# Two phases for the channel mixers, with the output product in Strassen's form

## What is computed

```python
def sq_relu_mlp(h, w1, w2):                 # w1 1024 x 4096, w2 4096 x 1024
    return jnp.square(jax.nn.relu(h @ w1)) @ w2
...
x = x + g2[:, None, :] * sq_relu_mlp(h, w_mlp_in[layer], w_mlp_out[layer])
```

## Time and profile before

| | |
|---|---|
| median of 3 runs | 3123.59 us (3119.03 to 3125.92) |
| profiled execution, span from first to last instruction | 3121.5 us |
| its own time beside the span | not recorded separately |
| TensorE busy | 3079.6 us, 99% |
| VectorE, ScalarE, GpSimd busy | 43%, 28%, 8% |

### The profile page before, as it was taken

How to read it: one execution, slowest core, us unless ns; L and a number is a source line. 1 busy time by engine, 2 the same in 40 slices (tenths; PEclk the granted TensorE clock), 3 DMA queues, 4 the chain that set the end, 5 groups by cost and what they waited for, 6 DMA issues and landing times.

```text
span 3121.5 us, 34385 instructions
## 1 busy us (share of the span) xinstructions
PE 3079.6 (99%) x13692; PEld 2479.9 (79%) x13692; DVE 1345.3 (43%) x1578; ACT 860.8 (28%) x1027; POOL 234.9 (8%) x352
## 2 busy tenths in 40 slices
PE   7999999999999999999999999999999999999999
PEld 5788888877777888888888778866767888888887
DVE  6664333255556333333336344255455533333333
ACT  5111222222233221111225344344244212221112
POOL 1000010000011000000011010123122000000000
PEclk8999999999999999999999999999999999999999
DMA  6655565533301111111113323455241111111111
GB/s 224 202 186 198 176 232 183 194 107 112 109 17 55 54 41 54 41 53 54 40 42 105 111 89 122 147 131 134 68 105 48 52 44 54 54 40 54 43 51 54
DMA packets 144669, 302.52 MB, mean 97 GB/s; under 512 B 10257, under 2 KB 72132, under 8 KB 144580
## 3 DMA queue, kind: packets, MB, share of 16 engines
q1 hardware_dynamic: 111220, 185.90, 18.4%
q0 software_dynamic: 33360, 115.38, 11.8%
HBM read 245.93 MB, written 55.18 MB: 96 GB/s over the span
## 4 chain that ended last, share of the span: by engine, by line
PE 93%; DVE 3%; ACT 2%; DMA 1%; issue 1%; POOL 0%; DVEq 0%; ACTq 0%; SPq 0%; POOLq 0%
PE ps L1572 10%; PE ps L1571 10%; PE ps L1568 10%; PE ps L1528 8%; PE ps L1531 8%; PE ps L1534 8%; PE ps L1686 5%; PE ps L1692 5%; PE ps L1689 5%; PE ps L1964 3%; PE ps L1660 3%; PE ps L1663 3%; PE ps L1664 3%; PE ps L1807 1%; PE ps L1779 1%; PE ps L1791 1%
## 5 line engine op out<-in xcount | busy, mean ns | idle before, releaser
L1568 PE MATMUL ps<-z_hi,w_hi 128*128 128x512 f32 x1408 | 552.0, 392 | 0.0
L1572 PE MATMUL ps<-z_hi,w_lo 128*128 128x512 f32 x1408 | 548.0, 389 | 0.0
L1571 PE MATMUL ps<-z_lo,w_hi 128*128 128x512 f32 x1408 | 547.9, 389 | 0.0
L1168 DVE SCALAR_TENSOR_TENSOR xT<-ps,ada,xT 128x512 f32<-128x512 f32 x352 | 259.2, 750 | 460.3 <-PE ps L1572 460.3
L1528 PE MATMUL ps<-h_hi,w_hi 128*128 128x512 f32 x1152 | 449.2, 390 | 2.7 <-DVE w_lo L1001 2.2
L1531 PE MATMUL ps<-h_lo,w_hi 128*128 128x512 f32 x1152 | 448.3, 389 | 0.0
L652 ACT ACTIVATE w_hi<-w_raw 128x2048 fp32r<-128x2048 f32 x116 | 221.5, 1909 | 736.5 <-PE ps L1568 487.7
L1534 PE MATMUL ps<-h_hi,w_lo 128*128 128x512 f32 x1152 | 354.6, 389 | 0.0
L1001 DVE TENSOR_TENSOR w_lo<-w_raw,w_hi 128x2048 fp32r<-128x2048 f32 x116 | 265.7, 2290 | 185.0 <-ACT w_hi L652 185.0
L1686 PE MATMUL ps<-h_hi,w_hi 128*128 128x512 f32 x768 | 303.4, 395 | 6.2 <-issue 2.0
L1571 PEld LDWEIGHTS ps<-z_lo,w_hi 128*128 128x128 f32 x1408 | 264.3, 188 | 56.7 <-issue 2.2
(11 more groups left out here) (268 smaller groups left out, 3625.9 us busy)
## 6 DMA issues: line engine op xcount, KB each, us to landing
misc<-w_ada SPq DMA_DIRECT2D x80, 512.0 KB, 5.1
w_raw<-w_mlp_in SPq DMA_DIRECT2D x32, 1024.0 KB, 5.5
w_raw<-w_mlp_out SPq DMA_DIRECT2D x32, 1024.0 KB, 5.1
w_raw<-ret_w_in SPq DMA_DIRECT2D x24, 1024.0 KB, 8.0
qk_s<-stage POOLq DMA_DIRECT2D x16, 512.0 KB, 3.9
v_s<-stage POOLq DMA_DIRECT2D x16, 512.0 KB, 3.8
g_s<-stage POOLq DMA_DIRECT2D x16, 512.0 KB, 3.5
misc<-kv_w_ada SPq DMA_DIRECT2D x16, 512.0 KB, 5.5
```

The source lines that it names most:

```text
L1168: STT(out=x_half, in0=bank[ring[q % 4]], scalar=ada[:, gate + q % 8:gate + q % 8 + 1], in1=x_half, op0=ALU.mult, op1=ALU.add).then_inc(d_f ...
L1568: mm = MM(out_bank, hi, z_hi[:, k, half(hf)], start=k == 0, stop=False)
L1571: MM(out_bank, hi, z_lo[:, k, half(hf)], start=False, stop=False)
L1572: mm = MM(out_bank, lo, z_hi[:, k, half(hf)], start=False, stop=k == 3)
```

## The change

The mixer now runs in two phases. In the first, all eight slices do their input product only; GpSimd issues a DMA that stores each squared middle tile (128 x 1024) to scratch `z_s`. In the second, the output product W2^T Z is taken over the contraction in slabs of 2 x `kh` tiles, `SLABS = (4, 4, 4, 2)`, so 28 of the 32 tiles. In a slab both operands are cut in 2 x 2 blocks (features and tokens in halves of 512, contraction in halves of `kh` tiles), and seven block products replace eight. Each product is 12 x `kh` matmuls in four banks; the banks alternate between lower and upper four. The eight block sums of a slab (four for each operand, up to 128 x 2048) are made by GpSimd, `sum_a` and `sum_b`. Operands and sums are split afresh, in pieces of 128 x 1024, four pieces of room for each operand, by ScalarE (`high`) and VectorE (`low`), two products ahead. VectorE adds each product's banks into `xT` at one or two places (`add_product`). The last four tiles go through `out_halves` as before, with middle tiles loaded back from scratch. Buffers `z_raw` and `a_raw` lie over the normalised input `h_hi`, `h_lo`, so their loads wait for the end of the first phase; two blocks of the weights go to `w_raw`, the first middle block to `low_tiles`.

```diff
-W_FK, W_FV = 64, 68
+W_FK, W_FV = 50, 54
...
+        SLABS = (4, 4, 4, 2)
+        NS, NP = len(SLABS), 7 * len(SLABS)
+        P_OF = [(b, i) for b in range(NS) for i in range(7)]
+        ADDS = (((0, 0),), ((0, 0),), ((0, 1),), ((1, 1),), ((1, 0), (1, 1)), ((0, 1),), ((1, 0),))
+        RING_X = 4
...
+        PROD_A, PROD_B = (0, 1, 5, 4, 2, 1, 3), (0, 2, 5, 4, 1, 3, 2)
+        SUM_A, SUM_B = {2: 2, 3: 1, 4: 3, 5: 4}, {2: 2, 3: 1, 4: 3, 6: 4}
...
@@ sync: loads @@
+                sp.wait_ge(xn_ready, 16 * (1, 4)[layer] + 16)
+                load_b(0, 0)
+                sp.wait_ge(lo_done, base + 15)
+                load_a(0, 0)
+                sp.wait_ge(lo_done, base + 16)
+                load_a(0, 1)
+                sp.wait_ge(a_full, a_end)
+                load_b(0, 2)
+                load_a(0, 2)
+                load_a(0, 3)
+                load_b(0, 1)
+                load_b(0, 3)
+                for b in range(1, NS):
+                    if b > 1:
+                        sp.wait_ge(sum_b_done, layer * 4 * NS + 4 * (b - 1) + 1)
+                        sp.wait_ge(ring_b_lo, split_done(layer, b - 1, 0))
+                    load_b(b, 0)
...
+                    sp.wait_ge(ring_b_lo, split_done(layer, b - 1, 6))
+                    load_b(b, 2)
+                    sp.wait_ge(ring_a_lo, split_done(layer, b - 1, 6))
+                    load_a(b, 3)
...
@@ gpsimd @@
+                for b, kh in enumerate(SLABS):
...
+                    sum_b(1, 4, 1, 0)
...
+                    sum_a(1, 4, 2, 3, ALU.add)
...
+                    sum_b(2, 5, 3, 4)
...
+                    sum_a(2, 5, 4, 0, ALU.subtract)
+                    sum_b(3, 1, 3, 1)
+                    sum_a(3, 2, 0, 2, ALU.subtract)
+                    pool.wait_ge(ring_a_lo, split_done(layer, b, 1))
+                    pool.wait_ge(sum_a_done, at + 2)
+                    sum_a(4, 1, 1, 5, ALU.subtract)
+                    pool.wait_ge(ring_b_lo, split_done(layer, b, 1))
+                    pool.wait_ge(sum_b_done, at + 2)
+                    sum_b(4, 2, 2, 5)
...
@@ vector @@
+                def low(n, which=(0, 1)):
+                    b, i = P_OF[n]
+                    for x, e in enumerate(pieces_of[n]):
+                        if x not in which:
+                            continue
+                        slot, cols = ring_of[e][0], slice(x * S, x * S + S)
+                        dve.wait_ge(ring_a_hi, layer * NE + e + 1)
+                        TT(ring_a(w_lo, slot), blk_a(PROD_A[i])[:, cols], ring_a(w_hi, slot).bitcast(F32),
+                           ALU.subtract).then_inc(ring_a_lo, 1)
...
+                for n in range(NP):
+                    if n + 2 < NP:
+                        low(n + 2, (0,))
+                    add_product(n)
+                    if n + 2 < NP:
+                        low(n + 2, (1,))
...
@@ tensor @@
+                def product(n):
+                    i, at = P_OF[n][1], (n + 1) % 2 * 4
+                    for e in pieces_of[n]:
+                        slot = ring_of[e][0]
+                        pe.wait_ge(ring_a_lo, layer * NE + e + 1)
+                        pe.wait_ge(ring_b_lo, layer * NE + e + 1)
+                        for k in range(2):
...
+                            for m in range(4):
+                                if first and n >= 2:
+                                    pe.wait_ge(o_read, layer * N_ADD + adds_of[n - 2, m][-1][2])
...
-                slice_(7, None, after)
-            mlp(W_MLP0, A_MLP0, D_MLP0, Z_MLP0, 1, sums_between(1), sums_after(2))
+                pe.wait_ge(d_free, d_base + 1)
+                for n in range(NP):
+                    if n == 1:
+                        pe.wait_ge(a_free, a_base + 32)
+                    product(n)
...
+                out_halves(w_base + 16, d_base, RING_MLP, 0, lambda hf, k: pe.wait_ge(z_lo_done, z_base + k + 1), then)
+            mlp(0, W_MLP0, A_MLP0, D_MLP0, Z_MLP0, 1, sums_between(1), sums_after(2))
```

More of the change, by code:

```diff
@@ new lines, in load_b @@
+                def load_b(b, n):
+                    kh, kp, th = SLABS[b], n // 2, n % 2
+                    kt = 8 * b + kh * kp
+                    for i in range(2):
+                        sp.wait_ge(z_spilled[i], layer * 256 + 16 * ((kt + kh) // 2))
+                    src = z_s[kt:kt + kh, :, half(th)]
+                    sp.dma_start(blk_b(b, n)[:, 0:kh * HALF].rearrange("p (k n) -> p k n", k=kh),
+                                 src.rearrange("k p n -> p k n")).then_inc(blk_b_loaded[n], 16)
@@ new lines, in mlp_loads @@
+                for i in range(2):
+                    sp.wait_ge(z_spilled[i], layer * 256 + 256)
+                for k in range(4):
+                    sp.dma_start(z_last[k], z_s[28 + k]).then_inc(z_last_loaded, 16)
+                sp.wait_ge(sum_a_done, layer * 4 * NS + 4 * NS)
+                sp.wait_ge(ring_a_lo, split_done(layer, NS - 1, 0))
+                load_pair(base + 16, 0, out_pair(w_mlp_out[layer], 28 * P, 0))
+                sp.wait_ge(ring_a_lo, split_done(layer, NS - 1, 5))
@@ L425, in _ @@
+                load_pair(base + 17, 1, out_pair(w_mlp_out[layer], 28 * P, 1), first=True)
             mlp_loads(W_MLP0, 0)
@@ L842, in slice_ @@
                           .then_inc(a_free, 1)
[L843 to L848, removed]
+                        if fin and j == 2:
+                            act.wait_ge(w_begun, w_base + 16)
+                            high(0)
@@ new lines, in z_high @@
+                def z_high(k):
+                    act.wait_ge(z_last_loaded, layer * 64 + 64)
+                    wait_piece_free(act, layer, holder[k])
+                    nc.scalar.activation(z_hi[:, k, :], z_last[k], ACT.Copy).then_inc(z_hi_done, 1)
+                slice_(7, fin=True)
+                act.wait_ge(a_full, a_base + 32)
+                for n in range(1, NP):
+                    high(n)
+                wait_piece_free(act, layer, holder[1])
+                prep(w_base + 16, 0, first=True)
@@ L1328, in slice_ @@
                         TT(sq_out[:, j % 2, :], relu_out[:, j % 2, :], relu_out[:, j % 2, :], ALU.mult)\
                             .then_inc(z_ready, 1)
[L1330 to L1337, removed]
+                        if fin and j == 2:
+                            low(0)
@@ new lines, in add_product @@
+                def add_product(n):
+                    at = (n + 1) % 2 * 4
+                    for m in range(4):
+                        dve.wait_ge(o_full, layer * 4 * NP + 4 * n + m + 1)
+                        for (mh, th), before, _ in adds_of[n, m]:
+                            if before:
+                                dve.wait_ge(o_read, layer * N_ADD + before)
+                            f = 4 * mh + m
+                            x_half = xT[:, f, half(th)]
+                            STT(out=x_half, in0=bank[at + m], scalar=ada[:, gate + f:gate + f + 1],
+                                in1=x_half, op0=ALU.mult, op1=ALU.add).then_inc(o_read, 1)
```

236 lines of the change are left out of this document (202 added, 34 removed).

## The result

The changed kernel takes 3160.14 us (median of 4 runs, 3156.12 to 3161.17) against 3121.96 us (4 runs, 3119.03 to 3125.92) for the kernel before, run beside it: a ratio of 1.0121, 95% interval 1.0106 to 1.0135. It is slower by 38 us. The profiled execution spans 3159.6 us and its own time is 3161.17, so 1.6 us lie around the span; the span grew by 38.1 us, where 37.0 was forecast.

What follows compares the result with a forecast made beforehand. TensorE, busy 99%, was taken to bound the kernel. A layer: -38.1 + 6.6 + 28.4 + 16.0 + 1.0 + 4.6 = +18.5 us, two +37.0; 3121.5 + 37.0 + 2.1 = 3160.6 us, range 3092 to 3180.

Steps and rivals of the forecast that it cites:

- Matmuls: Output product: seven block products replace eight, 168 matmuls fewer a layer, -38.1 us a layer, called sure.
- Seams: Input phase: TensorE waits 0.94 us for a bank evacuation at each of seven slice seams, +6.6 us a layer.
- First slab: Second phase's start: late loads and four sums stall product 2 by 22.7 us, its second half by 5.7; together 28.4.
- the walk: Step-by-step timing of loads, sums, splits and adds in the second phase's slabs, giving when product 2 can start.
- Slabs 1 and 2: VectorE splits wait out GpSimd sums: product 2 stalls 7.0 us, its second half 1.0; 8.0 a slab, 16.0 for two.
- Sum of 2048 columns: One GpSimd block sum in a full slab takes 4.7 us, between bounds of 2.3 and 5.2 us.
- Clock: TensorE at half rate after waits: 1.0 us in the first slab, 1.8 each in slabs 1 and 2; 4.6 a layer.
- Last slab and last 512: Second phase's end: the two-tile slab stalls 1 us (0 to 5), the final plain 512 stalls 0.
- a long sum lets VectorE in: Rival 1, second phase: VectorE gets in during a sum, so slabs 1 and 2 don't stall; 3098 us, chance 0.22.
- Short sums: Rival 2, second phase: GpSimd sums take only 2.3 to 3.9 us; 3085 us at 2.3; chance 0.12.
- Slow loads at the seam: Rival 3, first slab: each 1 MB load needs its lone 5.1 us, +7.2 us a layer, 3175 us; chance 0.08.
- VectorE alone binds: Rival 4, second phase: VectorE's own work limits; 56 of 76 us a slab says no; no chance given.

Runs made afterwards that it cites:

- run with fills: Changed kernel with block sums left out, products taking raw blocks, GpSimd filling an unused block twice per sum: 3090.11 us, 0.9895 of the kernel before.

## Why the prediction was right

The time was forecast at 3160.6 us and is 3160.14. The mechanism came as forecast; the closeness is partly luck, since errors of the sum cancel: 10.6 us too much waiting against 9.0 too little clock.

- **Matmuls**, -38.1 us a layer: 336 fewer in both layers, and what the run without sums gives (-59.5 in all) leaves no room for another size.
- **Seams**, +6.6: 7.2 by the run that removes them, 14 waits of the forecast size. The row of a similar seam elsewhere in the kernel gave the price of this one to a tenth.
- **First slab**, 22.7 us before product 2 and 5.7 in the middle: 23.4 and 2.65. The first was met by two wrong terms. The fourth load landed at 15.3 us and not at 13.2 (the windows at the start promised 390 GB/s behind the first load), and the four sums took 18.0 and not 18.8. The second was said too long mainly because the walk let the first half of product 2 run at full clock: it took 7.7 us in place of 5.45 (1346.95 to 1354.66), and those 2.3 us came off the wait. The other 0.9 are a start 0.6 us later than forecast and operands ready 0.3 us sooner.
- **Slabs 1 and 2**, 8.0 each: 5.5 and 6.0, nothing in the middle. Sums at 4.5 us undisturbed make a turn of 5.6 us where 5.9 was taken, and six of the seven sums are such turns.
- **Sum of 2048 columns**, 4.7 us: 4.5 to 4.6. The upper bound of four times the row of 512 columns was near, and the VectorE row (2.3 us) was rightly not. (The Trainium skill, GPSIMD Engine Reference, section 3.1, has 4.5 us, and the trace agrees.) By 4.5 us alone the sum was said to be 9 us lower. The idle time came out 10.6 us lower (39.9 against 45.4 us in the first layer, 40.3 in the second), but about 4 of these are the exchange of waiting for clock in the first slab.
- **Clock**, 4.6 us a layer: 10.5 and 7.7. This is the mis-sized term. I took 1.8 us for a wait in slabs 1 and 2 and 1.0 for the first slab, on the ground that the second wait there would swallow most. It did swallow the 2.1 behind the first wait, which are booked here and missing there, but was followed by 1.7 of its own; slabs 1 and 2 lost 2.3 and 2.6, and the last 512 lost 1.8 where nothing was put. Without the 2.1 the loss is 8.4 us in the first layer against 4.6. It was within its bounds of 0 to 11.
- **Last slab and last 512**, 1 and 0: 0 and 2.4 us of waiting, with 1.8 of clock behind it in the first layer.

For the first layer: -38.1 + 7.2 + 39.9 + 10.5 = 19.5 us. The stretch from the mixer's first ReLU copy to the next phase grew by 20.6 us (698.92 to 719.53); 1.1 us stay unassigned. The rest of the program with the second mixer grew by 19.6 us (17.1 by the same sum, 2.5 unassigned), less 2.1 us that the start of this execution was shorter: 38.1 in all.

The rivals: *a long sum lets VectorE in* is refuted by splits of 5.5 us; its price for the first slab alone (14.7 us) was fair: the run with fills has 12.36 there with a chain 3.6 us shorter. (It starts from 32.4 where the walk gives 32.0.) *Short sums* is refuted by the row of 4.5 us, though cutting them into pieces takes most of the waits of slabs 1 and 2 away, as it said of short sums. *Slow loads at the seam* is true to 2.1 of its 7.2 us, and not for its reason, as the last section shows. *VectorE alone binds* is refuted by the run without sums. And the point at which the change was said to cost nothing, a sum of 3.9 us, can't be read from a run: the runs with pieces change the turn and keep the chain.

## What to carry to other kernels

A busy share of 8 or 50% says nothing about room when two engines share a port: cost a GpSimd operation with two SBUF inputs as time taken from VectorE too, one whole instruction for each turn, and keep such instructions short, with a wait between them. Where a chain of loads and sums has nothing to hide behind, give its first links to the engine that idles there, and load first what that engine needs. A wait of TensorE of a few microseconds costs some 2 us more in its clock (1.7 to 2.6 here behind waits of 2.65 us and more; behind 1.8 us it was 1.8 once and nothing once), so price the number of waits besides their length.

## What was not expected of the hardware

- Fifteen GpSimd operations of 512 columns, one right behind the other, kept VectorE's split out for 19.45 us, in both layers (19.46); with pieces of 1024 or 2048 columns the engines alternated, and with a wait on its own piece GpSimd gave a turn after each (split 2.29 us).
- A GpSimd operation that only writes (1.81 us for 2048 columns) does not slow VectorE's two-input split at all: 1.22 us beside it.
- The loads at the seam took 15.3 us for four blocks of 1 MB, where the forecast had 13.2. The first landed as forecast: ScalarE's copy of it starts at 1306.96, 5.1 us behind the seam. The 2.1 us are in the next three, 3.4 us each in place of 2.7. In the run without sums the first and third operation of GpSimd, which wait for the fourth and the fifth load, start at 1316.31 and 1318.91, 2.6 us apart, so the step of 2.7 holds there. The second and the third share the DMA engines with the store of the last middle tile (512 KB, issued at 1304.80), which the forecast left out; at the forecast's 390 GB/s that is 1.3 us, an estimate. The rest stays open.
